# A two-layer encoder trunk on one core: one queue for the opening, and two turns of each feed-forward issued from ScalarE

## The chip, the core and the metric

The kernel runs on one NeuronCore of one Trainium2 chip. A core has five engines with a list of instructions each, which run side by side and wait for one another on semaphores: TensorE (PE, matmuls and transposes), VectorE (DVE), ScalarE (ACT), GpSimd (POOL) and SyncE (SP), which here only issues DMAs. SP and ACT have a DMA queue each (q1 and q10 in the profile); both feed the same 16 DMA engines. The metric is the time of one execution in microseconds on the device; lower is better. Times inside the program are given in us from the start of the profiled span.

## What is computed

The trunk has two layers over 256 rows (frames) of 1024 features. Each layer is a feed-forward with half weight, a mixer (convolution and attention side by side, merged by gates), and a second such feed-forward. Cut to what the change touches:

```python
D_MODEL = 1024; SEQ = 256; DEPTH = 2; D_FF = 2816
def _rms_norm(x, g):
    y = x * lax.rsqrt(jnp.mean(x * x, axis=-1, keepdims=True) + EPS)
    return y * g
def _swiglu(h, w_gate, w_up, w_down):
    return (jax.nn.silu(h @ w_gate) * (h @ w_up)) @ w_down
for l in range(DEPTH):
    x = x + 0.5 * _swiglu(_rms_norm(x, ffn1_norm[l]), ffn1_w_gate[l], ffn1_w_up[l], ffn1_w_down[l])
    ...  # mixer
    x = x + 0.5 * _swiglu(_rms_norm(x, ffn2_norm[l]), ffn2_w_gate[l], ffn2_w_up[l], ffn2_w_down[l])
```

## The kernel before

**Tiles and units.** The 256 rows are two tiles (t = 0, 1) of 128. A feed-forward runs over 11 chunks (NCH, c = 0 to 10) of 256 of the 2816 inner columns. Weights come in units of 128 partitions x 2048 floats, 1 MB each. A chunk has three units: gate and up for rows 0 to 511 of the features (half h = 0), the same for rows 512 to 1023 (h = 1), and down. A feed-forward is 33 units. Units 0 and 1 are chunk 0's gate and up, 2 and 3 chunk 1's, 4 is chunk 0's down, then 5, 6 (chunk 2's), 7 (chunk 1's down), and so on. In each half-unit of the opening, a quarter (q = 0, 1) is two blocks of 128 feature rows.

**Every product is three.** Weights and activations are float32 and each is split into a rounded part (whi, hThi, gThi) and its rest (wlo, hTlo, gTlo). TensorE forms hi x hi, hi x lo and lo x hi. So a unit goes through: a DMA into one of three raw slots (SP, `place`, L360), rounding on ACT (`split`, L1044, semaphore whi_ready), the rest on DVE (`split`, L1390, semaphore wlo_ready), and then the matmuls. SP may send unit u when wlo of unit u - 3 is done, since that frees the slot. The rounding of unit u waits for its landing and for a slot among six rounded ones (unit_free).

**The turn.** What a chunk gives (silu of gate times up, one 128 x 256 tile per t) must be transposed before the product with down. ACT splits its 32-bit words into two planes of 16 bits (`split_planes`, L1110), a DMA transpose turns both tiles at once (`plane_turn`, L385, issued by SP), DVE joins the planes again (`join`, L1478), ACT rounds (`round_joined`, L1118), DVE forms the rest gTlo (`rest_joined`, L1395), and PE may start the products with down. Chunks 0 to 9 are turned so, 40 in all over the four feed-forwards. Chunk 10 is turned by TensorE (`turn`, L716), since nothing is left to cover the DMA. Each turn waits for the join of the one before, as planes and turned are single buffers.

**Order.** Each engine's order is written out by hand, nothing is scheduled. PE does gate_up of chunk c for both tiles (24 matmuls each), then down of chunk c - 1 for both (12 each). At the end it does gate_up of chunk 10 for tile 0, half of that for tile 1, turn of chunk 10 for tile 0, down of chunk 9 for tile 0, down of chunk 10 for tile 0. ACT's `first` (L1130) has, behind the silu of tile 1 of chunk 0, the split of unit 4 and then the planes of tile 1. SP sends the turn of chunk c - 2 between the two gate-up units of chunk c and the down unit; the turn of chunk 9 is sent where the next part's first unit has been sent: after the gain, vec, qkg and first w_in loads of the mixer (L429), or after the first unit of the next layer (L400).

**The opening.** x comes in four pieces of 128 x 512. Tile 0's first piece is SP's first DMA, the second comes from ACT (L1350). Units 0 and 1 are sent in quarters, gate by SP and up by ACT (`first_unit`, L329), and x's second tile by both (`second_tile`). TensorE turns x by 128 x 128 blocks (L645), ACT rounds these with the gain as scale (`gained_round`, L1071), DVE forms the rest (`gained_rest`, L1440). PE's `first_gate_up` (L689) takes for each half tile 0 in two quarters, then tile 1 in one piece of four blocks. `keep_busy` is a number of matmuls on zeros whose result nobody reads. `factors` turns the gains into columns.

## Time and profile before

| | |
|---|---|
| runs shown, us | 1063.89, 1064.58, 1068.48; median 1064.58 |
| profiled execution, us | 1062.78, span 1060.9 |
| TensorE matmul busy | 1048.6 us (99%), 5100 instructions |
| VectorE, ScalarE, GpSimd busy | 673.2 us (63%), 560.1 us (53%), 229.5 us (22%) |
| DMA | 205.06 MB, mean 193 GB/s; q1 (SP) 61.3%, q10 (ACT) 1.2% of 16 engines' span |
| granted TensorE clock, mean over the span | 1.0 of full speed |
| split of a unit, ACT L1044 | 178 times, mean 1908 ns |
| low part of a unit, DVE L1390 | 154 times, mean 2286 ns |

How to read it: with an engine at 99% of the span, the time outside its work is what can still be saved. It has to be looked for in single places, where PE stood and something else released it. Busy time of the others tells only whether they have room; how they are ordered decides when PE gets its operands.

### The profile page before, as it was taken

What the parts mean: (1) busy time and instruction counts of PE and PEld (TensorE: products, weight loads), DVE (VectorE), ACT (ScalarE), POOL (GpSimd) and SP (SyncE); (2) the same over time, 40 slices, a digit from 0 to 9 for tenths busy, and PEclk for the clock granted to TensorE, in tenths of its full rate; (3) what the DMA queues carried; (4) which work ended last, traced back from release to release, by engine and by line L of the source; (5) the groups of instructions that cost most, each with busy time, mean ns of one, the idle gap of its engine ahead of it and who ended that gap; (6) DMA issues with size and microseconds to landing.
All of it is one profiled execution on the core that took longest, in us unless ns stands there. A gap on an engine that the chain in (4) does not pass through costs nothing. (4 is left out here: it accounts for less than half of the span.)

```text
span 1060.9 us, 13912 instructions
## 1 busy us (share of the span) xinstructions
PE 1048.6 (99%) x5100; PEld 878.8 (83%) x5100; DVE 673.2 (63%) x899; ACT 560.1 (53%) x732; POOL 229.5 (22%) x258
## 2 busy tenths in 40 slices
PE   8999999999999999999999999999999999999998
PEld 5888887998888888888888888879988887888887
DVE  6556556599976465565656546556999665564563
ACT  6445445575762554454455535536767535454461
POOL 1840000049850000000048000002589300000000
PEclk9999999999999999999999999999999999999999
DMA  8776786365645367767656686674366345867761
GB/s 277 220 230 202 211 242 225 127 219 169 208 149 179 95 203 218 225 200 219 217 159 204 186 249 204 206 247 157 132 209 232 105 159 129 220 203 220 225 203 48
DMA packets 176701, 205.06 MB, mean 193 GB/s; under 512 B 49264, under 2 KB 147856, under 8 KB 176656
## 3 DMA queue, kind: packets, MB, share of 16 engines
q1 hardware_dynamic: 174064, 200.78, 61.3%
q10 hardware_dynamic: 2592, 3.69, 1.2%
q8 instruction: 27, 0.44, 0.2%
q14 instruction: 18, 0.15, 0.0%
HBM read 192.90 MB, written 1.05 MB: 183 GB/s over the span
## 5 line engine op out<-in xcount | busy, mean ns | idle before, releaser
L1390 DVE TENSOR_TENSOR wlo<-raw,whi 128x2048 fp32r<-128x2048 f32 x154 | 351.4, 2286 | 69.1 <-ACT whi L1044 69.0
L604 PE MATMUL bank<-whi,hThi 128*128 128x512 f32 (+1 forms) x976 | 379.2, 388 | 0.3 <-DVE wlo L1390 0.3
L606 PE MATMUL bank<-whi,hTlo 128*128 128x512 f32 (+1 forms) x976 | 373.7, 383 | 0.0
L605 PE MATMUL bank<-wlo,hThi 128*128 128x512 f32 (+1 forms) x976 | 373.6, 383 | 0.0
L1044 ACT ACTIVATE whi<-raw 128x2048 fp32r<-128x2048 f32 x178 | 338.7, 1908 | 16.2 <-DMA raw<-in_ffn_w_up 7.9
L604 PEld LDWEIGHTS bank<-whi,hThi 128*128 128x128 f32 x976 | 183.4, 188 | 36.0 <-DVE wlo L1390 0.7
L606 PEld LDWEIGHTS bank<-whi,hTlo 128*128 128x128 f32 x976 | 183.2, 188 | 35.8
L605 PEld LDWEIGHTS bank<-wlo,hThi 128*128 128x128 f32 x976 | 183.5, 188 | 34.2
L1118 ACT ACTIVATE gThi<-vtok 128x512 fp32r<-128x512 f32 x40 | 25.3, 632 | 277.1 <-DVE vtok L1478 237.8
L604 PE MATMUL bank<-whi,gThi 128*128 128x512 f32 (+1 forms) x416 | 162.7, 391 | 2.7 <-DVE gTlo L1395 2.7
L605 PE MATMUL bank<-wlo,gThi 128*128 128x512 f32 (+1 forms) x416 | 161.2, 387 | 0.0
L606 PE MATMUL bank<-whi,gTlo 128*128 128x512 f32 (+1 forms) x416 | 161.2, 387 | 0.0
L472 POOL TENSOR_TENSOR small<-small,expo 128x1 f32<-128x1 f32 (+3 forms) x20 | 21.7, 1087 | 602.6 <-DVE small L1399 562.5
L1478 DVE COPY vtok<-qkT 128x1024 uint16<-128x1024 uint16 x40 | 30.2, 755 | 166.6 <-DMA qkT<-qkT 166.4
L586 POOL TENSOR_TENSOR wlo<-raw,whi 128x2048 fp32r<-128x2048 f32 x24 | 110.2, 4604 | 19.1 <-ACT whi L1044 18.8
L1557 DVE SCALAR_TENSOR_TENSOR bank<-cu,vec,bank 128x256 f32<-128x256 f32 x240 | 97.3, 484 | 0.1
L604 PEld LDWEIGHTS bank<-whi,gThi 128*128 128x128 f32 x416 | 78.1, 188 | 19.7 <-DVE gTlo L1395 4.3
L606 PEld LDWEIGHTS bank<-whi,gTlo 128*128 128x128 f32 x416 | 78.1, 188 | 16.1
L605 PEld LDWEIGHTS bank<-wlo,gThi 128*128 128x128 f32 x416 | 78.2, 188 | 15.3
L1110 ACT ACTIVATE qkT<-gates 128x512 uint16<-128x512 uint16 x80 | 50.0, 625 | 23.9 <-DVE gates L1465 23.9
L1101 ACT ACTIVATE gates<-bank,small 128x256 f32<-128x256 f32 x88 | 40.5, 460 | 19.1 <-PE bank L606 17.8
L1395 DVE TENSOR_TENSOR gTlo<-vtok,gThi 128x512 fp32r<-128x512 f32 x40 | 27.7, 692 | 35.5 <-ACT gThi L1118 35.5
(163 smaller groups left out, 805.8 us busy)
## 6 DMA issues: line engine op xcount, KB each, us to landing
raw<-in_ffn_w_down SPq DMA_DIRECT2D x88, 512.0 KB, 5.4
raw<-in_ffn_w_gate SPq DMA_DIRECT2D x86, 512.0 KB, 4.2
raw<-in_ffn_w_up SPq DMA_DIRECT2D x86, 512.0 KB, 5.3
raw<-in_w_in SPq DMA_DIRECT2D x48, 512.0 KB, 4.9
raw<-in_w_out SPq DMA_DIRECT2D x16, 512.0 KB, 4.4
raw<-in_w_in SPq DMA_DIRECT2D x8, 544.0 KB, 7.6
raw<-in_w_mla_out SPq DMA_DIRECT2D x8, 512.0 KB, 3.9
raw<-in_w_conv_out SPq DMA_DIRECT2D x8, 512.0 KB, 4.8
```

The lines of the kernel that those rows point to most:

```text
L586: nc.gpsimd.tensor_tensor(wlo[:, slot(u, RING), 0:n], raw[:, slot(u, RAW), 0:n], whi[:, slot(u, RING), 0:n].bitcast(F32), ALU.subtract).th ...
L604: nc.tensor.matmul(out, lh, rh, start=start, stop=False, skip_group_check=skip)
L605: nc.tensor.matmul(out, lh, rl, start=False, stop=False, skip_group_check=skip)
L606: return nc.tensor.matmul(out, ll, rh, start=False, stop=stop, skip_group_check=skip)
L1044: nc.scalar.activation(whi[:, slot(u0, RING), 0:USED[u0]], raw[:, slot(u0, RAW), 0:USED[u0]], ACT.Copy).then_inc(whi_ready, 1)
L1101: nc.scalar.activation(sgate[:, t, :], bank[:, 4 + t, 0:FC], ACT.Silu, scale=rs[:, t:t + 1]).then_inc(silu_ready, 1)
L1110: nc.scalar.activation(planes[:, :, :, t, :], words, ACT.Copy).then_inc(planes_ready, 1)
L1118: nc.scalar.activation(gThi[:, (c0 % 2) * 2:(c0 % 2) * 2 + 2, :], g_turned.rearrange("p (k n) -> p k n", k=2), ACT.Copy).then_inc(ghi, 2)
L1390: nc.vector.tensor_tensor(wlo[:, slot(u0, RING), 0:n], raw[:, slot(u0, RAW), 0:n], whi[:, slot(u0, RING), 0:n].bitcast(F32), ALU.subtract) ...
L1395: return nc.vector.tensor_tensor(out, in_, hi.bitcast(F32), ALU.subtract)
L1478: nc.vector.tensor_copy(g_turned.bitcast(U16).rearrange("p (n b) -> p b n", b=2), turned.rearrange("p (b j) r -> p b (j r)", b=2)).then_in ...
L1557: ins = nc.vector.scalar_tensor_tensor(out=o, in0=i, scalar=w, in1=o, op0=ALU.mult, op1=ALU.add)
```

## The change

**Opening, DMAs.** SP issues all of x and all of units 0 and 1; ACT issues none of them and keeps only the two small loads of gains. The order is: x tile 0 half 0, quarter (0, 0) as gate and up, x tile 1 half 0, quarter (0, 1), x tile 0 half 1, quarter (1, 0), x tile 1 half 1, quarter (1, 1). A new semaphore x_second marks x tile 1 half 0.

**Opening, order of work.** Each quarter is used for tile 0 and then for tile 1. For tile 1 the term with hTlo comes last. The transposes of x are now four at a time (`first_turn`), each into a bank of its own per tile (`norm_bank`). ACT and DVE alternate a half of a tile of x and a quarter of a unit. keep_busy between the first transposes and the next has 10 matmuls in place of 5. The squares of tile 0 on DVE (`first_squares`) go from its first place to behind the first quarter of unit 1.

**Turns.** The turns of chunks 0 and 9 of each feed-forward (8 of 40) are issued by ACT, right behind the planes. In `first` the planes of tile 1 and the turn stand ahead of the split of unit 4, not behind it. The turns of chunks 1 to 8 stay with SP.

```diff
@@ x and units 0 and 1, on SP
-        def first_unit(eng, h, g):
-        def second_tile(eng, h):
...
+            def x_half(t, h, landed):
+                sp.dma_start(x[:, t, h * 512:(h + 1) * 512],
+                             a["x"][0, t * P:(t + 1) * P, h * 512:(h + 1) * 512]).then_inc(landed, 16)
+            def first_quarter(h, q, landed):
+                u0 = unit_gu(0, 0, h)
+                dst = raw[:, slot(u0, RAW), 0:2048].rearrange("p (k g n) -> p k g n", k=4, g=2)
+                rows = slice((4 * h + 2 * q) * P, (4 * h + 2 * q + 2) * P)
+                sp.wait_ge(wlo_ready, u0 + 1)
+                for g, w in enumerate((wg[0], wu[0])):
+                    sp.dma_start(dst[:, 2 * q:2 * q + 2, g, :],
+                                 w[0, rows, 0:FC].rearrange("(k p) n -> p k n", p=P)).then_inc(landed, 16)
...
-                        first_unit(sp, 0, 0)
-                        second_tile(sp, 0)
-                        first_unit(sp, 1, 0)
+                        for h in range(2):
+                            if h:
+                                x_half(0, 1, x_landed[0])
+                            first_quarter(h, 0, first_landed[h])
+                            x_half(1, h, x_landed[1] if h else x_second)
+                            first_quarter(h, 1, raw_landed[slot(unit_gu(0, 0, h), RAW)])
@@ turns no longer on SP
-                        if f == 0:
-                            plane_turn(l - 1, 1, NCH - 2)
...
-                    if c > 1:
+                    if c > 2:
                         plane_turn(l, f, c - 2)
...
-                    if h == 1:
-                        plane_turn(l, 0, NCH - 2)
...
-            plane_turn(DEPTH - 1, 1, NCH - 2)
@@ first_products(t, h, q) on PE
+                    term(hThi, whi, first=True)
+                    if t == 0:
+                        pe.wait_ge(nlo, per_norm_half(0, 0, t, h))
+                        term(hTlo, whi)
...
+                    ins = term(hThi, wlo, last=t == 0)
+                    if t == 1:
+                        pe.wait_ge(nlo, per_norm_half(0, 0, t, h))
+                        ins = term(hTlo, whi, last=True)
@@ first_gate_up on PE
+                            ins = first_products(0, h, q)
+                            if (h, q) == (0, 1):
+                                first_turn(1, 1)
+                                turn_factors(1)
+                            elif (h, q) == (1, 1):
+                                ins.then_inc(gu_done, 1)
+                            ins = first_products(1, h, q)
+                            if (h, q) == (0, 0):
+                                first_turn(0, 1)
...
-                        norm(l, n, 0)
-                        keep_busy(5)
+                        first_turn(0, 0)
+                        keep_busy(10)
+                        first_turn(1, 0)
@@ turns on ACT
+                def plane_turn(c):
+                    act.wait_ge(planes_ready, per_turn(l, f, c) * TT)
+                    act.wait_ge(joined, per_turn(l, f, c))
+                    act.dma_start_transpose(turned[:, :, :], planes.rearrange("p b k t f -> p (b k t f)")
+                                            ).then_inc(turned_landed, 16)
...
                     silu(0, 1)
+                    split_planes(0, 1)
+                    plane_turn(0)
                     split(l, UB[f] + 4)
-                    split_planes(0, 1)
...
                 pair(NCH - 2, NCH - 2)
+                plane_turn(NCH - 2)
@@ ACT's opening
-            act.dma_start(x[:, 0, 512:D], a["x"][0, 0:P, 512:D]).then_inc(x_landed[0], 16)
...
-            first_unit(act, 0, 1)
-            second_tile(act, 1)
-            first_unit(act, 1, 1)
...
+                    for h in range(2):
+                        gained_round(0, 0, 0, h)
+                        first_split(h, 0)
+                        gained_round(0, 0, 1, h)
+                        first_split(h, 1)
@@ DVE's opening
+                    for h in range(2):
+                        gained_rest(0, 0, 0, h)
+                        first_split(h, 0)
+                        if h:
+                            first_squares()
+                        gained_rest(0, 0, 1, h)
+                        if h:
+                            norm_scale(0, 0, 0)
+                        first_split(h, 1)
```

How it moves instructions. TensorE's list from the first transposes of x to the first transposes of its second tile, before (bank<-ident,x is a transpose of x, bank<-zero is keep_busy, L676 are the first products):

```order
L645 MATMUL bank<-ident,x 128x128 x8
L611 MATMUL bank<-zero 128x512 x5
L676 MATMUL bank<-whi,hThi 128x512 x2
L676 MATMUL bank<-whi,hTlo 128x512 x2
L676 MATMUL bank<-wlo,hThi 128x512 x2
```

And the same place in the changed kernel, where these lines have the numbers L683, L618 and L692:

```order
L683 MATMUL bank<-ident,x 128x128 x4
L618 MATMUL bank<-zero 128x512 x10
L683 MATMUL bank<-ident,x 128x128 x4
L692 MATMUL bank<-whi,hThi 128x512 x2
L692 MATMUL bank<-whi,hTlo 128x512 x2
L692 MATMUL bank<-wlo,hThi 128x512 x2
L692 MATMUL bank<-whi,hThi 128x512 x2
L692 MATMUL bank<-wlo,hThi 128x512 x2
L692 MATMUL bank<-whi,hTlo 128x512 x2
```

Four transposes of tile 0 have left the place ahead of the products, four of tile 1 have come there, and tile 1 follows tile 0 on the same quarter. ScalarE's list around chunk 0 of a feed-forward before (gates<-bank is silu, qkT<-gates are the planes, whi<-raw of 2048 a split of a unit):

```order
L1101 ACTIVATE gates<-bank,small 128x256
L1052 ACTIVATE htok,small<-x 128x1024
L1044 ACTIVATE whi<-raw 128x2048
L1110 ACTIVATE qkT<-gates 128x4x128
L1101 ACTIVATE gates<-bank,small 128x256
L1044 ACTIVATE whi<-raw 128x2048
L1110 ACTIVATE qkT<-gates 128x4x128
```

And now, with the waits printed, in the changed kernel:

```order
L1124 ACTIVATE gates<-bank,small 128x256 [waits rs_ready,gu_done]
L1074 ACTIVATE htok,small<-x 128x1024 [waits x_landed1,x_second,x_new]
L1065 ACTIVATE whi<-raw 128x2048 [waits unit_free,raw_landed0]
L1133 ACTIVATE qkT<-gates 128x4x128 [waits gu_ready]
L1124 ACTIVATE gates<-bank,small 128x256 [waits rs_ready,unit_free]
L1133 ACTIVATE qkT<-gates 128x4x128 [waits gu_ready]
L1140 DMA_TRANSPOSE qkT<-qkT 128x8x128 [waits joined,planes_ready]
L1065 ACTIVATE whi<-raw 128x2048 [waits unit_free,raw_landed1]
```

The second planes have moved ahead of the second split, and the issue of the turn stands between them. SyncE's list at the start of a mixer loses the turn of chunk 9 between the two pairs of w_in; before:

```order
L360 DMA raw<-in_w_in 128x2x544 x2
L385 DMA_TRANSPOSE qkT<-qkT 128x8x128
L360 DMA raw<-in_w_in 128x2x544 x2
```

## Rows read from the trace of the kernel before

**Rows 1.** Waits of TensorE, whole span: us in total, times, longest us.
```profile
PE bank L604 <- DVE gTlo L1395: 2.7, 4, 0.8
```

**Rows 2.** Timeline of the opening: start us, us, engine, work [idle before <-releaser].
```profile
3.76 1.73 PE L645 MATMUL bank<-ident,x 128*128 128x128 f32 x8
...
5.18 0.84 ACTq L1341 DMA_DIRECT2D cacc<-in_ffn_norm  x1
...
5.33 1.24 PE L611 MATMUL bank<-zero 128*128 128x512 bf16 x5
...
6.35 1.14 ACT L1071 ACTIVATE hThi<-bank,fgain 128x128 fp32r<-128x128 f32 x4
...
7.91 1.06 ACT L1063 ACTIVATE whi<-raw 128x1024 fp32r<-128x1024 f32 x1 [0.42 <-DMA raw<-in_ffn_w_up]
8.99 1.22 DVE L1424 TENSOR_TENSOR wlo<-raw,whi 128x1024 fp32r<-128x1024 f32 x1 [0.34 <-ACT whi L1063]
...
9.11 0.70 PE L676 MATMUL bank<-whi,hThi 128*128 128x512 f32 x2 [2.53 <-ACT whi L1063]
```

**Rows 3.** Timeline, end of the opening's products and turn of chunk 0.
```profile
20.50 0.48 ACT L1101 ACTIVATE gates<-bank,small 128x256 f32<-128x256 f32 x1 [1.27 <-PE bank L676]
...
22.12 1.07 PE L676 MATMUL bank<-wlo,hThi 128*128 128x512 f32 x4
...
26.06 0.48 DVE L1465 SCALAR_TENSOR_TENSOR gates<-bank,small,gates 128x256 f32<-128x256 f32 x1
...
26.20 0.50 PE L604 MATMUL bank<-whi,hThi 128*128 128x512 f32 x1 [0.29 <-DVE wlo L1390]
...
26.54 2.29 DVE L1390 TENSOR_TENSOR wlo<-raw,whi 128x2048 fp32r<-128x2048 f32 x1
...
32.73 0.76 DVE L1478 COPY vtok<-qkT 128x1024 uint16<-128x1024 uint16 x1 [3.90 <-DMA qkT<-qkT]
...
35.15 0.50 PE L604 MATMUL bank<-whi,gThi 128*128 128x512 f32 x1 [0.49 <-DVE gTlo L1395]
```

**Rows 4.** Timelines by engine, turn of chunk 9, layer 1's first feed-forward.
```profile
689.99 0.61 ACT L1110 ACTIVATE qkT<-gates 128x512 uint16<-128x512 uint16 x1
...
690.84 3.40 SPq L385 DMA_TRANSPOSE qkT<-qkT  x1
...
700.07 0.75 DVE L1478 COPY vtok<-qkT 128x1024 uint16<-128x1024 uint16 x1 [4.30 <-DMA qkT<-qkT]
...
702.78 0.44 PE L716 MATMUL bank<-ident,gates 128*128 128x128 f32 x2 [1.59 <-DVE gates L1465]
...
706.65 0.50 PE L604 MATMUL bank<-whi,gThi 128*128 128x512 f32 x1 [0.68 <-DVE gTlo L1395]
```

**Rows 5.** Timelines by engine, the same turn in layer 0.
```profile
168.86 2.23 SPq L385 DMA_TRANSPOSE qkT<-qkT  x1
...
176.91 0.75 DVE L1478 COPY vtok<-qkT 128x1024 uint16<-128x1024 uint16 x1 [3.94 <-DMA qkT<-qkT]
...
183.50 0.50 PE L604 MATMUL bank<-whi,gThi 128*128 128x512 f32 x1 [0.68 <-DVE gTlo L1395]
```

**Rows 6.** Timelines by engine, turns of chunk 0: layer 1's first, then last feed-forward.
```profile
556.87 0.39 PE L604 MATMUL bank<-whi,gThi 128*128 128x512 f32 x1
...
888.26 0.48 DVE L1465 SCALAR_TENSOR_TENSOR gates<-bank,small,gates 128x256 f32<-128x256 f32 x1
...
890.27 1.25 SPq L385 DMA_TRANSPOSE qkT<-qkT  x1
...
899.09 0.50 PE L604 MATMUL bank<-whi,gThi 128*128 128x512 f32 x1 [0.80 <-DVE gTlo L1395]
```

**Rows 7.** Source line of the turns: issue in ns, then landing, min/median/max.
```profile
L385 SPq DMA_TRANSPOSE qkT<-qkT x40: 1232/2048/3403, 27.2 to 1032.9; - x40
...
DMA to landing us min/median/max: 3.0/6.2/9.2
```

**Rows 8.** Stretch 5 to 12 us: busy of engines, PEclk, DMA share, GB/s.
```profile
5.00:12.00 7.00, 4.47 (x19) 2.35 (x17) 4.47 (x9) 4.47 (x11) 0.00 (x0) 1.00 1.05 353
```

More of the change, by code:

```diff
@@ L194, in trunk @@
         x_first = sem("x_first")
+        x_second = sem("x_second")
         gain_landed = sem("gain_landed")
@@ L670, in gate_up, with first_turn @@
                             between()
-                def first_products(t, u, ks, wait_rest, wait_low):
-                    def term(left, right, k, start, stop):
-                        return nc.tensor.matmul(bank[:, 4 + t, :], left[:, 4 * u + k, t * P:(t + 1) * P],
-                                                view(right, u, 2048, 4)[:, k, :], start=start, stop=stop)
-                    for k in ks:
-                        term(hThi, whi, k, u == 0 and k == 0, False)
-                    wait_rest()
-                    for k in ks:
-                        term(hTlo, whi, k, False, False)
-                    wait_low()
-                    for k in ks:
-                        ins = term(hThi, wlo, k, False, u == 1 and k == 3)
+                def first_turn(t, h):
+                    pe.wait_ge((x_first, x_second)[t] if h == 0 else x_landed[t], 16)
+                    if h:
+                        pe.wait_ge(nlo, per_norm_half(0, 0, t, 0))
+                    for k in range(4):
+                        ins = nc.tensor.transpose(bank[:, norm_bank(0, 0, t, h), k * P:(k + 1) * P],
+                                                  x[:, t, (4 * h + k) * P:(4 * h + k + 1) * P], ident[:, :])
+                    ins.then_inc(ntr, 1)
@@ new lines, in first_products, with term @@
+                def first_products(t, h, q):
+                    def term(left, right, first=False, last=False):
+                        for k in (2 * q, 2 * q + 1):
+                            ins = nc.tensor.matmul(bank[:, 4 + t, :], left[:, 4 * h + k, t * P:(t + 1) * P],
+                                                   view(right, h, 2048, 4)[:, k, :],
+                                                   start=first and (h, k) == (0, 0), stop=last and (h, k) == (1, 3))
+                        return ins
+                    pe.wait_ge(nhi, per_norm_half(0, 0, t, h))
+                    if q == 0:
+                        pe.wait_ge(first_hi, h + 1)
+                    else:
+                        pe.wait_ge(whi_ready, h + 1)
+                    term(hThi, whi, first=True)
+                    if t == 0:
+                        pe.wait_ge(nlo, per_norm_half(0, 0, t, h))
+                        term(hTlo, whi)
+                    if q == 0:
+                        pe.wait_ge(first_lo, h + 1)
+                    else:
+                        unit_waits(pe, 0, h)
+                    ins = term(hThi, wlo, last=t == 0)
+                    if t == 1:
+                        pe.wait_ge(nlo, per_norm_half(0, 0, t, h))
+                        ins = term(hTlo, whi, last=True)
```

60 lines of the change are left out of this document (12 added, 48 removed).

## The prediction, made before the changed kernel ran

> **What bounds the kernel now.** I read the shares of the page first: TensorE (PE) is busy 1048.6 us of a span of 1060.9, so this change can win only what PE does not work. Next the waits of PE alone over the whole span [rows 1]: nearly all of it in four waits for gTlo, 2.7 us. Beside them the timeline shows 2.53 us before the first product [rows 2] and 1.59 us for the product to be turned in layer 1 [rows 4]. To the idle time of such a row 0.16 us are added, because matmuls stand 0.227 us apart while their modelled length is 0.39 (four in 1.07, [rows 3]); the four gTlo waits and the last named then cost 0.65, 0.84, 0.84, 0.96 and about 1.6 us. Everything else is TensorE's own pace. So two places count: the opening up to 35.15 us, and the turn (DMA transpose) of the first and the last-but-one chunk of a feed-forward.
>
> **Opening, the start.** PE's first useful matmul begins at 9.11 us [rows 2]. Behind it stands ACT: its queue issued eight transfers before it computed, the last from 5.18 to 6.02 us, so the first rounding of x (1.14 us for four tiles) starts at 6.35 although its transposes lay in PSUM by 4.9; then the first split of weights waited for the up quarter until 7.91. In the changed kernel ACT issues two small transfers, and SP sends everything. Rounding then starts at 4.9 and ends at 6.0. Ahead of the first pair of quarters' end there are 768 KB (half a tile of x, gate, up). The chip moved 353 GB/s from 5 to 12 us [rows 8]: three quarters of a MB at that rate take 2.2 us; from about 2.5 us and with half a us for landing I estimate 5.2, and up to 6 with a slow start. The split (1.06) is then done at 7.0 to 7.1. But PE is not there yet: keep_busy grows from 5 to 10 matmuls. They begin at 4.6, where PE's transposes still stand 0.21 apart (8 in 1.73), two at 0.42, the rest at the 0.22 of [rows 2] (5 in 1.24), so until 7.1; four transposes follow. First product at 7.6: 1.5 us earlier than now, and it is PE's own list that sets it, which also covers a landing up to 0.5 us late.
>
> **Opening, the middle.** One pass over a quarter for one tile is six matmuls, 1.37 us; eight passes are 10.9 us, with 12 transposes and the factor's in between 1.5 us. Per quarter, with its two passes of 1.37, ACT has one group of roundings and one split, 1.14 + 1.06 = 2.2 us, DVE as long a group and 1.22, 2.35 us, and once the squares, about one split more [rows 2]. Both keep up, with stalls of some 0.2 us where the rest of x for tile 1 comes last (that is why its term is put last). I get the end of the first products at 20.2 (7.6 + 10.9 + 1.5 + 0.2). Before, it is 23.03 (four matmuls from 22.12, [rows 3]). The second unit's low part is ready at 20.45 (DVE's chain from 14.6: squares, group, 1.22, 2.29, each about as now), so chunk 1 begins at 20.5, **2.5 us early**.
>
> **Opening, what is late next.** This does not stay. Silu of tile 0 sits on ACT ahead of the split of unit 3, and from its start at 20.50 to the first product with unit 3 at 26.20 there are 5.7 us [rows 3]. In the changed kernel tile 0's gate_up ends at 18.9 instead of 20.3, so silu starts at 19.1 and unit 3 is ready at 24.8; PE arrives at 23.2 and stands 1.6 us. **1.4 us early** is left. Then comes the turn: the product of tile 1 follows that low part by 0.4 us as at 26.06 now (25.2), its planes take 0.6 (25.8), the issue on ACT, t = 1.25 us (27.1), the split of unit 4, 1.90 (29.0), its low part, 2.29 (31.3), and only then DVE's join, since the split stands ahead of it in DVE's list; join to first product is 32.73 to 35.15, 2.42 us. That gives 33.7, against 33.0 at which PE is there and 35.15 now: **opening 1.45 us**. The turn itself has landed by then (25.8 + 5.5 as now = 31.3).
>
> **Price of an issue on ACT.** No row shows a turn issued there. On SP it takes 1.23 to 3.40 us, 2.05 in the middle [rows 7]. The long ones stand behind loads of weights in the same queue; at 1.25 [rows 6] SP had issued nothing for a while. ACT's queue is empty outside the mixer, so I take 1.25 and keep 3.4 as upper end. It pushes the split that follows and its low part on DVE, and through them the join.
>
> **Last-but-one turns (four).** In layer 1's first feed-forward SP issues vectors, gains and w_in, then the turn at 690.84, which takes it 3.40 us; it lands 9.2 us later, DVE starts at 700.07, PE waits 1.6 us for the product and 0.84 for gTlo [rows 4]. The planes are ready at 690.6. From ACT: issue to 691.9, split 1.9, low part 2.3, so the join can start at 696.1 if the turn lands within 5.5 us. That is 3.9 us earlier. The product of the last chunk then waits only for its own matmuls: PE is at the turn at 701.0 (702.78 less 1.75) and done with tile 0 twelve matmuls before, at 698.3; silu and mul, half a us each, are over at 699.5: both stalls go, **2.4 us**. In layer 0 the same turn is issued at 168.86 and joined from 176.91 on [rows 5]; the join comes at 174.3 instead, and the 0.84 us before 183.50 go: **0.85 us**. In the two second feed-forwards no wait of PE hangs on it ([rows 1] has four gTlo waits in all, and all four are named here): gain and loss zero; if an issue of 3.4 us pushed them, some us lie between gTlo and its use.
>
> **First turns (the other three).** The planes are split before unit 4's split instead of after it, 0.86 us earlier: in the last feed-forward mul is done at 888.74 [rows 6], planes at 889.4, issue to 890.65, split, low part to 894.9; join no later than 895.8 is needed for PE at 898.13, and the turn lands by then even with the present 6.4 us. The 0.96 us before 899.09 go: **0.95 us**. The other two have no wait now; by the same sum their gTlo comes at 374.1 and 555.9, where PE wants it at 375.0 and 556.9. Slack 0.9 us each, so t up to 2.2 is free (PE's row of the second is in [rows 6]). Unit 7's load is issued 2.8 us later than now in each; ACT wants it some 11 us after that.
>
> **Sum.** 1.45 + 2.4 + 0.85 + 0.95 = 5.65 us, against the profiled execution: 1062.78 (span 1060.9) to 1057.1. That execution was 1.8 us below the median of the runs shown, 1064.58; the same difference from the median gives 1059.0 us. As a function of t: gain = 6.9 - t up to 2.2 us, and 13.5 - 4t above, because four first turns then lie on PE's path; from 2.8 on the last-but-one turns give less too. It is zero near 3.2.
>
> **A rule against it.** The layer-1 turn stood 9.2 us behind other loads [rows 4]; the sum takes it that a queue of its own ends this. DMA: Bandwidth & Descriptors of the Trainium skill (Issuing engines are not separate DMA queues) says that transfers started by different engines run on the same 16 DMA engines and interleave, so only the sequencer's time is saved; the same page (Queues, rings and completion order) says that each engine goes round the queues packet by packet. By the second the turn passes the waiting loads, as the sum has it; by the first it would land little sooner, and the sum would be that of rival (1). No row here decides it.
>
> **Rivals.**
> (1) The turns land no sooner from ACT, because their packets share the engines with w_in. For: the chip is busy there. Against: the turn that had little else beside it landed in 3.0 us, the best of forty [rows 7]. Then 2.4 + 0.85 fall away: gain 2.4, 1062.2 us. Chance 0.15.
> (2) The opening wins nothing: a single queue brings the first quarters as late as now (7.9), the first product is at 9.1, and everything in the opening shifts by 1.5 us. Gain 4.2, 1060.4 us. For: today two queues fill the start, and one may not. Against: later, SP's queue alone carries all weights, and the two share the engines now. Chance 0.12.
> (3) **Slower**: the issue on ACT is long, as SP's longest, 3.4 us or more. Then the first turns of all four feed-forwards are late through split, low part and join, more than the last-but-one turns give back: at 3.4 the opening loses 0.7, two first turns 1.2 each and the last 0.25, the last-but-one still give 2.25: 1.1 us slower, 1065.7 us, and 4 to 6 us more per us beyond. It decides from t = 3.2. Against: ACT's queue holds nothing else. Chance 0.06.
> (4) The opening keeps its 2.5 us, because split and low part of unit 3 run into less: gain 6.7, 1057.9 us. Chance 0.10.
>
> **How the numbers follow.** The forecast has 0.57, with its own range 4.4 to 6.8 us of gain, 1057.8 to 1060.2. Faster by over 0.5% (5.3 us; about what a measurement of this kernel can tell from no change) means below 1059.3: rather more than two thirds of the forecast's part and all of (4), 0.50. Within 0.5%: the rest of it, (1), (2) and most of (3), 0.45. Slower 0.05. The range leaves out the ends of (3) and (4) and allows for the spread of the runs, 1063.9 to 1068.5 before: 1056.0 to 1064.5.
>
> **What would show it.** First product at 7.6 (late landing: over 8.5); chunk 1's first matmul at 20.5 and a wait of 1.6 us before unit 3; down of chunk 0 at 33.7. A turn's issue on ACT of 1.2 to 1.3 us. No wait of PE for the product in layer 1, none for gTlo at the last-but-one turns and the last feed-forward. Wrong would be: PE waits for gTlo or the low part of unit 4 in the middle feed-forwards, or a turn from ACT landing after 7 us.

## The result, and the profile of the changed kernel

The changed kernel takes 1071.22 us (median of 20 runs, 1058.41 to 1075.74) against 1063.96 (20 runs of the kernel before, 1060.25 to 1068.48). The ratio is 1.0059, 95% interval 1.0043 to 1.0075: slower by 0.6%, where 1059.0 was forecast. The profiled execution took 1072.15 us with a span of 1070.3; that of the kernel before had a span of 1060.9. Two of the 20 runs (1058.41 and 1062.65 us, mean granted clock 1.000 and 0.998 against 0.995 in the profiled one) show little or nothing of the loss; they left no trace that would say why.

TensorE's waits over the whole span (us in total, times, longest):

```profile
PE bank L736 <- DVE gates L1492: 9.2, 2, 4.8
PE bank L611 <- DVE gTlo L1421: 1.2, 2, 0.7
...
PE bank L611 <- DVE wlo L1416: 1.0, 1, 1.0
PE bank L683 <- DMA x<-in_x: 1.0, 1, 1.0
```

Two of the four gTlo waits of [rows 1] are gone; the forecast had a third one gone too, that of the last feed-forward. In their place stand two waits for the product that PE is to turn, 9.2 us together, or 4.6 and 5.0 with the 0.16 us that the prediction adds to each. Both stand ahead of a mixer, where the turn of chunk 9 is under way. Timelines by engine there, layer 0 and then layer 1 (start us, us, engine, work, idle before and its releaser):

```profile
168.60 2.12 ACTq L1140 DMA_TRANSPOSE qkT<-qkT  x1
...
170.40 5.88 SPq L355 DMA_DIRECT2D raw<-in_w_in  x4
...
181.06 0.74 DVE L1505 COPY vtok<-qkT 128x1024 uint16<-128x1024 uint16 x1 [6.00 <-DMA qkT<-qkT]
...
183.76 0.69 PE L736 MATMUL bank<-ident,gates 128*128 128x128 f32 x2 [4.43 <-DVE gates L1492]
...
696.36 2.87 ACTq L1140 DMA_TRANSPOSE qkT<-qkT  x1
...
709.20 0.74 DVE L1505 COPY vtok<-qkT 128x1024 uint16<-128x1024 uint16 x1 [5.62 <-DMA qkT<-qkT]
...
711.89 0.69 PE L736 MATMUL bank<-ident,gates 128*128 128x128 f32 x2 [4.79 <-DVE gates L1492]
```

From issue to join are now 12.5 and 12.8 us; in [rows 5] and [rows 4] they were 8.1 and 9.2. The turn is issued right behind its planes as before, and from issue to join it takes 4.4 and 3.6 us longer. DVE's mul of the last chunk stands behind this join in DVE's list, and PE's transpose of that product stands ahead of the last products with down: so all of PE waits.

The wait costs more than itself. Stretches around the two places (busy us of PE with its instructions in brackets, then the other engines; behind them the granted clock, DMA share, GB/s):

```profile
179.00:184.00 5.00, 0.57 (x3) 0.24 (x2) 1.83 (x3) 2.12 (x3) 0.00 (x0) 0.85 0.90 206
184.00:190.00 6.00, 6.00 (x17) 4.79 (x17) 5.09 (x3) 2.96 (x3) 0.00 (x0) 0.56 0.25 66
190.00:200.00 10.00, 10.00 (x51) 8.30 (x51) 3.48 (x5) 2.25 (x5) 0.57 (x1) 1.00 0.40 146
706.00:712.00 6.00, 1.21 (x6) 0.67 (x5) 1.82 (x3) 1.98 (x3) 0.00 (x0) 0.96 1.00 255
712.00:716.00 4.00, 4.00 (x13) 3.25 (x14) 3.05 (x3) 3.10 (x3) 0.00 (x0) 0.63 0.05 19
716.00:726.00 10.00, 10.00 (x47) 8.20 (x46) 5.52 (x6) 2.01 (x4) 0.57 (x1) 1.00 0.55 184
...
183.70:185.70 2.00, 1.94 (x6) 1.66 (x7) 0.89 (x2) 2.00 (x3) 0.00 (x0) 0.50 0.04 11
711.90:713.90 2.00, 2.00 (x6) 1.71 (x7) 0.95 (x1) 2.00 (x3) 0.00 (x0) 0.50 0.12 43
```

Right behind each wait the granted clock is 0.50, the lower of its two levels (1.2 of 2.4 GHz); the stretches of 6 and 4 us hold 0.56 and 0.63 because it rises to 1.00 within them. In 184 to 190 there are 17 matmuls where the next stretch has 30.6 per 6 us, so 13.6 matmuls' time, 2.7 us, is missing; in 712 to 716 there are 13 against 18.8, which is 1.2 us. Waits of 9.5 and clock of 3.9 make 13.4 us. Less the waits that were there before (1.6 + 0.84 + 0.84 at the same two places) some 10 us are left. The spans of the two executions differ by 9.4, so these two places account for the whole loss.

The opening, in rows of its timeline:

```profile
4.84 1.14 ACT L1093 ACTIVATE hThi<-bank,fgain 128x128 fp32r<-128x128 f32 x4 [1.21 <-PE bank L683]
5.86 1.07 ACT L1085 ACTIVATE whi<-raw 128x1024 fp32r<-128x1024 f32 x1
...
8.07 0.66 PE L683 MATMUL bank<-ident,x 128*128 128x128 f32 x4 [0.95 <-DMA x<-in_x]
8.49 0.71 PE L692 MATMUL bank<-whi,hThi 128*128 128x512 f32 x2
...
21.84 0.47 PE L611 MATMUL bank<-whi,hThi 128*128 128x512 f32 x1 [0.37 <-DVE gates L1492]
...
25.84 0.50 PE L611 MATMUL bank<-whi,hThi 128*128 128x512 f32 x1 [1.02 <-DVE wlo L1416]
...
34.86 0.50 PE L611 MATMUL bank<-whi,gThi 128*128 128x512 f32 x1 [0.54 <-DVE gTlo L1421]
```

Rounding at 4.84 and the split over by 6.93 came as forecast (4.9 and 7.0). But x's tile 1, half 0, landed at 8.03 (of its 16 completion marks in the trace the first came at 5.72), and its four transposes stand ahead of the first product: 8.49 instead of 7.6. All later steps are 1.0 to 1.3 us behind the forecast: chunk 1 at 21.84 (20.5), unit 3 at 25.84 (24.8), down of chunk 0 at 34.86 (33.7; before 35.15). The wait before unit 3 is 1.02 us, where 1.6 was forecast.

The page of the line of ACT's turns (issue in ns, then landing in us, minimum, median, maximum):

```profile
L1140 ACTq DMA_TRANSPOSE qkT<-qkT x8: 1256/1298/2870, 26.9 to 1042.3; - x8
...
DMA to landing us min/median/max: 3.1/6.1/12.8
```

The issue costs ACT 1.3 us, as taken (t = 1.25). It is the landing that goes above 12 us: 12.4 us in layer 0, 12.8 in layer 1.

### The profile page after: what moved, and what is told of

Read it like the earlier page. It is cut to its first block, busy times and chain, and to the rows that moved or that the text cites. A ratio compares the mean times of both kernels' runs of the same rounds, so it can differ in the third digit from the quotient of the medians.

```text
span 1070.3 us, 13927 instructions
## 1 busy us (share of the span) xinstructions
PE 1052.8 (98%) x5105; PEld 882.1 (82%) x5105; DVE 672.5 (63%) x899; ACT 561.9 (52%) x732; POOL 230.7 (22%) x258
## 4 chain that ended last, share of the span: by engine, by line
PE 91%; DMA 4%; ACT 2%; DVE 1%; issue 1%; ACTq 0%; POOL 0%; SPq 0%; DVEq 0%
PE bank L611 28%; PE bank L612 28%; PE bank L613 28%; DMA qkT<-qkT 3%; PE bank L692 1%; ACT whi L1065 1%; PE bank L650 1%; PE bank L844 1%; PE bank L856 1%; DMA x<-in_x 1%; ACT htok L1074 0%; PE bank L876 0%; PE bank L877 0%; PE bank L855 0%; PE bank L1030 0%
```

## Experiments

The span of one profiled execution is a poor measure here, because the opening scatters from execution to execution: the down of chunk 0 begins anywhere between 35.15 and 37.65 us in five profiled executions with the old opening (e4, with chunk 0's turn on ACT, among them), and between 34.28 and 36.83 in eight with the new (three of them with chunk 0's turn on SP). The table therefore has, beside the ratio, the part from there to the end of the span (span less the start of that row), and the time from the end of the turn's planes to the start of its join in layers 0 and 1. Span and what stands right of it are from one execution each.

| kernel | median us | ratio to before, 95% | span | down of chunk 0 at | rest | planes to join, us |
|---|---|---|---|---|---|---|
| before | 1063.96 | 1 | 1060.9 | 35.15 | 1025.8 | 8.1, 9.5 |
| changed | 1071.22 | 1.0059 [1.0043, 1.0075] | 1070.3 | 34.86 | 1035.4 | 12.5, 12.9 |
| e1_last_on_sp | 1062.74 | 0.9993 [0.9979, 1.0008] | 1058.5 | 35.16 | 1023.3 | 6.6, 9.1 |
| e2_opening_only | 1062.68 | 0.9991 [0.9976, 1.0007] | 1057.1 | 34.74 | 1022.4 | 6.4, 8.0 |
| e3_last_only | 1073.46 | 1.0086 [1.0070, 1.0102] | 1074.0 | 37.56 | 1036.4 | 13.3, 12.8 |
| e4_first_only | 1063.63 | 1.0006 [0.9990, 1.0021] | 1063.8 | 37.65 | 1026.2 | 9.2, 9.0 |
| e5_hold_w_in | 1059.57 | 0.9990 [0.9977, 1.0003] | 1055.5 | 34.28 | 1021.2 | 6.5, 7.0 |
| e6_vec_later | 1059.09 | 0.9985 [0.9968, 1.0003] | 1055.3 | 34.31 | 1021.0 | 5.6, 5.6 |
| e7_hold_vec_later | 1058.55 | 0.9969 [0.9957, 0.9980] | 1057.7 | 36.72 | 1021.0 | 5.7, 5.6 |
| e8_sp_vec_later | 1058.51 | 0.9968 [0.9956, 0.9980] | 1056.9 | 34.69 | 1022.2 | 4.9, 7.5 |
| e9_turn_behind | 1069.35 | 1.0060 [1.0041, 1.0080] | 1069.1 | 35.27 | 1033.8 | 11.5, 12.4 |
| e10_vec_only | 1059.60 | 0.9976 [0.9961, 0.9990] | 1057.8 | 36.50 | 1021.3 | 5.5, 5.0 |
| e11_x_ahead | 1059.00 | 0.9968 [0.9955, 0.9980] | 1057.9 | 36.83 | 1021.1 | 4.5, 4.5 |

Three groups were run, each with its own runs of the kernel before beside it: e1 to e4 (1063.47), e5 to e8 (1061.36), e9 to e11 (1061.72, on another chip than the other runs). Medians of different groups are not compared, ratios are.

### Which part loses: e1 to e4

**e1_last_on_sp.** The changed kernel with the turns of chunk 9 back on SP at their old places:

```diff
                 pair(NCH - 2, NCH - 2)
-                plane_turn(NCH - 2)
...
                 for h in range(2):
+                    if h == 1:
+                        plane_turn(l, 0, NCH - 2)
                     block_of(l, UM + M_PR + h, a["w_in"], 4 * h * P, 4, O1, PR)
```

> The changed kernel with the turns of chunk 9 issued by SyncE again, in their old places; opening and the turns of chunk 0 stay as changed. Theory (shared engines): the changed kernel lost its time at two turns alone, those of chunk 9 ahead of a mixer, which landed 12.5 and 12.8 us after their issue on ScalarE (8.0 and 9.2 from SyncE before), because SyncE's w_in load that used to stand behind them in one queue now runs beside them. Then this kernel has no wait of TensorE over 2 us at the product to be turned and ends near the kernel before, from 3 us under it to 1 us over: ratio 0.997 to 1.001. Rival (opening or turns of chunk 0 cost the time): it stays 4 us or more over the kernel before, ratio 1.004 or more.

Measured 0.9993 [0.9979, 1.0008], as the theory has it, and the longest PE wait for the product is 1.1 us. The other three are the kernel before with one part each. **e2_opening_only** has the opening's DMAs and PE, ACT and DVE order of the change, all turns on SP:

> The kernel before with the changed opening alone; all 40 turns from SyncE at their old places. In the changed kernel the down product of chunk 0 began at 34.86 us against 35.15, so the opening looks worth 0.3 us with the turn of chunk 0 on ScalarE. Theory: on its own it is worth 0 to 1.5 us, ratio 0.9985 to 1.0; with the turn back on SyncE the first split of unit 4 is earlier. Rival (the rearranged opening also shifts later loads so that turns land later): over 1.002.

Measured 0.9991 [0.9976, 1.0007]: inside the theory's range, and not told from no change. **e3_last_only** has the turns of chunk 9 on ACT (the lines of e1's diff the other way round):

> The kernel before with the four turns of chunk 9 issued from ScalarE and nothing else. Theory: this part alone carries the whole loss: turns ahead of the mixers land 12 to 13 us after issue, TensorE waits 4 to 5 us at the product to be turned in both layers and then runs some 12 matmuls 0.43 us apart; 8 to 10 us slower than before, ratio 1.008 to 1.0095. Rival (the loss needs the opening or the turns of chunk 0 beside it, through a shifted phase of loads): under 1.003. The prediction's own view was 3 us faster, 0.997.

Measured 1.0086 [1.0070, 1.0102], with waits of PE of 5.4 and 4.9 us for the product to be turned, as expected. **e4_first_only** has the turns of chunk 0 on ACT, with the planes ahead of unit 4's split:

> The kernel before with the four turns of chunk 0 issued from ScalarE, planes ahead of the split of unit 4, nothing else. Issue 1.25 to 1.35 us. Theory: it lands no sooner than from SyncE (5.6 to 7.1 us), the split of unit 4 comes 2.9 us later, the slack of 0.5 to 1 us is used up, TensorE gains nothing: 0 to 1 us slower, ratio 1.000 to 1.001. Rival (as predicted): the wait before the down product of the last feed-forward goes, 1 us faster, 0.999.

Measured 1.0006 [0.9990, 1.0021]; the turns land 5.7 to 6.8 us after their issue. So the loss is the move of chunk 9's turns, it is there without the opening and the first turns, and nothing is seen of a worth of the turns of chunk 0. One thing does not add up: the move alone costs 1.0086, the whole change 1.0059, each beyond the other's interval. The opening (0.9991) makes good a third of that; the rest is not explained.

### Why the turn lands late: e5 to e8

Two things stand out in the trace of the changed kernel. First, the turn was issued at 168.60, and for nearly five us not one packet of ACT's queue (q10) moves; nor does much else. DMA of the stretch 168.6 to 173.5 (busy tenths of the engines in 40 slices, GB/s in the same slices, then packets, MB and share of the one queue that has any):

```profile
DMA  9622110000000000000022539798999999999999
GB/s 291 184 75 85 38 28 10 4 6 8 5 8 4 6 12 8 14 10 16 16 46 67 138 133 315 273 392 322 463 355 409 391 409 426 409 444 373 462 373 409
...
q1 hardware_dynamic: 800, 0.91, 51.7%
```

From about 169 to 171 the DMA engines are nearly idle. What trickles there are the q and k norm rows, which SP issued from 165.02 on, each sent to all 128 partitions: the trace has 128-byte packets, 24 to 53 in each half us. This is no different in the kernel before: its turn was issued at 168.86 and had its first packet at 174.55, and from 169.5 to 171.5 its engines moved 17 GB/s. Second, when q10's packets come, they run beside the second unit of w_in, which SP issued from 170.40 on; in the kernel before the turn stood ahead of that unit in the same queue. This is new. Stretch 174 to 177.5 of the changed kernel, then 179 to 183 of e3_last_only (queue: packets, MB, share):

```profile
q1 hardware_dynamic: 532, 1.09, 89.0%
q10 hardware_dynamic: 531, 0.14, 20.2%
```

```profile
q1 hardware_dynamic: 697, 1.31, 86.9%
q10 hardware_dynamic: 716, 0.18, 21.1%
```

Both queues get nearly the same number of packets, 532 to 531 and 697 to 716; but q1's have up to 2176 bytes and q10's 256, so the turn gets about an eighth of the bytes. In layer 1 the counts are less even (339 to 509 in 702 to 706 of the changed kernel). Theory A is this sharing, theory B the small loads.

**e5_hold_w_in** takes the sharing away: SP sends the second unit only when the turn has landed.

```diff
                 for h in range(2):
+                    if h == 1:
+                        sp.wait_ge(turned_landed, per_turn(l, 0, NCH - 2) * 16)
                     block_of(l, UM + M_PR + h, a["w_in"], 4 * h * P, 4, O1, PR)
```

> The changed kernel; ahead of the second w_in unit of each mixer SyncE now waits until the turn of chunk 9 has landed. In the changed kernel that unit was issued 1.8 us after the turn and ran beside it; the DMA engines gave each queue one packet in turn (697 packets of SyncE's queue to 716 of ScalarE's in 4 us of the run with the last turns alone on ScalarE), 2176-byte packets against 256-byte ones. Theory A (equal packets, and the unit behind is what the turn shares with): the turn lands 7.5 to 9.5 us after issue as it did from SyncE, the waits of 4.8 and 4.4 us shrink under 2 us, ratio 0.998 to 1.002. Theory B (small loads ahead, vec and the q and k norms, hold the start of the turn's packets, 5 us after issue): the landing hardly moves, over 11 us, ratio 1.005 or more.

```profile
167.99 1.86 ACTq L1142 DMA_TRANSPOSE qkT<-qkT  x1
174.47 0.76 DVE L1507 COPY vtok<-qkT 128x1024 uint16<-128x1024 uint16 x1 [0.28 <-DMA qkT<-qkT]
178.58 0.38 PE L738 MATMUL bank<-ident,gates 128*128 128x128 f32 x2
```

The join comes 6.5 us after the issue (7.0 in layer 1), PE does not wait (no idle time on its row), and the ratio is 0.9990. This is theory A's ratio, with a landing still sooner than its 7.5 us, and against theory B.

**e6_vec_later** takes the small loads away instead: the vector row and the q and k norms go behind both units, and the sharing is left possible.

```diff
-                sp.wait_ge(vec_used, l + 1)
-                sp.dma_start(vec[:, :], a["vec"][l]).then_inc(vec_landed, 16)
-                for n, w in enumerate((a["q_norm"], a["k_norm"])):
-                    sp.dma_start(qkg[:, n, :], w[bass.ds(l, 1), NOPE:QK].to_broadcast([P, ROPE])).then_inc(vec_landed, 16)
                 for h in range(2):
                     block_of(l, UM + M_PR + h, a["w_in"], 4 * h * P, 4, O1, PR)
+                sp.wait_ge(vec_used, l + 1)
+                sp.dma_start(vec[:, :], a["vec"][l]).then_inc(vec_landed, 16)
+                for n, w in enumerate((a["q_norm"], a["k_norm"])):
+                    sp.dma_start(qkg[:, n, :], w[bass.ds(l, 1), NOPE:QK].to_broadcast([P, ROPE])).then_inc(vec_landed, 16)
```

> The changed kernel with the loads of vec and of the q and k norms sent behind the two w_in units of the mixer instead of ahead of them. In the trace of the changed kernel the DMA engines moved next to nothing for 2 us while these loads' 128-byte packets went out, and the turn's first packet came 5 us after its issue. Theory B: packets of the turn start 1.5 to 3 us after issue, landing 6 to 9 us, ratio 0.997 to 1.002. Theory A (only the unit beside it counts): the small loads cost 1 to 2 us at most, the turn still shares with 2.2 MB of w_in and lands after 10 us or more, ratio 1.003 to 1.006.

```profile
168.03 1.27 ACTq L1141 DMA_TRANSPOSE qkT<-qkT  x1
173.56 0.75 DVE L1506 COPY vtok<-qkT 128x1024 uint16<-128x1024 uint16 x1
```

Its queues in 168.6 to 171.6:

```profile
q10 hardware_dynamic: 1056, 0.26, 56.3%
q1 hardware_dynamic: 201, 0.40, 52.9%
```

Now q10's first packet comes 1.2 us after the issue, q10 has over half of the engines' time in this stretch, the issue is the short one, and the join starts without idle time in front of it: DVE's own list, not the landing, sets it. In the trace the turn has landed at 171.66, 3.6 us after its issue, sooner than the 6 us of theory B. Alone, this experiment would have been taken for theory B; e5 shows that holding the unit back is enough too.

**e7_hold_vec_later** has both edits, **e8_sp_vec_later** has e6's edit with all turns on SP (opening as changed).

> Both edits on the changed kernel: small loads behind the w_in units, and the second unit held until the turn has landed. Whatever the parts are, both theories together leave the turn little beside it: landing 4 to 6 us after issue, no wait of TensorE for the product to be turned, 2 to 4 us faster than the kernel before, ratio 0.996 to 0.998. If it stays above 1.001 there is a third cause in ScalarE's queue itself.

> The changed opening, all turns from SyncE at their old places, and the small loads behind the two w_in units of the mixer. The turn of chunk 9 then stands behind one w_in unit alone. Theory B: it lands 4.5 to 6 us after issue instead of 8 to 9, both waits before the last chunk's products go (0.8 us in layer 0, 2.4 us in layer 1), ratio 0.995 to 0.998 against the kernel before, 2 to 3 us under the run with the opening alone. Theory A: the turn is behind w_in as before, landing 7 us or more, ratio as with the opening alone, 0.999.

Both measured the same, 0.9969 and 0.9968: 0.3% faster than the kernel before. With e11 they have the lowest ratios of the study. In e8's layer 1 the issue still took 3.11 us and the join came 7.5 us after it, longer than theory B had it, but no PE wait hung on it. The two causes act in series rather than add up: without the sharing planes-to-join falls from 12.5 to 6.5 us, without the small loads to 5.6, without both to 5.7.

Where the turn's packets stand among those of w_in can be counted in the traces. A turn has 1024 packets of 256 bytes, each w_in unit 512 of 2176. Layer 0, then layer 1:

| kernel | first packet of the turn after its issue, us | w_in packets started before it | from its first to its last packet, us |
|---|---|---|---|
| before | 5.7, 5.5 | 449, 313 | 1.8, 3.2 |
| changed | 5.2, 4.2 | 431, 286 | 6.4, 7.9 |
| e3_last_only | 5.3, 4.8 | 145, 294 | 7.4, 7.2 |
| e5_hold_w_in | 3.5, 2.8 | 428, 384 | 2.4, 3.6 |
| e6_vec_later | 1.2, 1.2 | 462, 470 | 1.9, 2.1 |
| e7_hold_vec_later | 3.0, 2.3 | 457, 451 | 1.9, 1.8 |
| e9_turn_behind (below) | 5.1, 5.1 | 922, 856 | 2.6, 3.6 |

The change left the first packet nearly where it was and stretched the rest from 1.8 and 3.2 us to 6.4 and 7.9: this is the loss. It also shows that ACT's queue did not take the turn past the first unit, which SP had issued before. In layer 0 of e7, with no small loads in the way, the turn was issued at 170.44, 0.12 us before the first packet of that unit moved, and its own first packet still came at 173.40, behind 457 of the 512. So the small loads need not hold ACT's queue themselves; they hold up the first unit, and the turn's packets come when a good part of that unit has gone (more than half, in all rows but those of e3). In e6 it was nearly gone 1.2 us after the issue, and the turn was through before the second unit's packets came. Which engine issues the turn makes no difference that e7 and e8 show, once the small loads are out of the way.

### Which order in one queue: e9 to e11

**e9_turn_behind** asks whether a second queue is needed for the harm at all: the kernel before, the turn moved on SP from ahead of the second unit to behind it.

```diff
                 for h in range(2):
-                    if h == 1:
-                        plane_turn(l, 0, NCH - 2)
                     block_of(l, UM + M_PR + h, a["w_in"], 4 * h * P, 4, O1, PR)
+                    if h == 1:
+                        plane_turn(l, 0, NCH - 2)
```

> The kernel before, with one line moved: SP still issues the turn of chunk 9 in the mixers, but behind the second unit of w_in instead of ahead of it. Asks whether the place against that unit alone costs, with no second queue in it. Theory (order on the line, not the queue's owner, decides): the turn's packets come behind all of that unit, so issue to join is 8 to 11 us from the issue, and the issue itself comes later by the two issues of the unit; the join is at 180 us or later in layer 0 and 708 or later in layer 1 (before: 176.91 and 700.07), TensorE stands 3 to 6 us at each of the two products, loss 4 to 10 us, 1066 to 1072 us where before gives 1062.5, ratio 1.004 to 1.009. Rival (a second queue is what hurts, the packets of two queues in turn): within one queue the turn loses at most 2 us, TensorE stands under 1.5 us each, ratio 1.000 to 1.002. The first feed-forward's other turns are as before.

```profile
172.18 1.92 SPq L385 DMA_TRANSPOSE qkT<-qkT  x1
180.48 0.74 DVE L1478 COPY vtok<-qkT 128x1024 uint16<-128x1024 uint16 x1 [7.35 <-DMA qkT<-qkT]
183.18 0.69 PE L716 MATMUL bank<-ident,gates 128*128 128x128 f32 x2 [3.41 <-DVE gates L1465]
...
710.69 0.44 PE L716 MATMUL bank<-ident,gates 128*128 128x128 f32 x2 [4.29 <-DVE gates L1465]
```

1.0060 [1.0041, 1.0080], as the theory has it: a loss like that of the change (1.0059), with one queue only. The closer comparison is e3, which also has nothing but the move, to ACT: 1.0086 [1.0070, 1.0102], the intervals just overlap, so a second queue may cost a little more. Planes to join are 11.5 and 12.4 us here, 12.5 and 12.9 in the changed kernel. A turn that ACT's own queue got at 168.60 is no sooner joined (181.06) than one that SP issued at 172.18 behind both units (180.48). The ways differ, since here the turn is issued 3.3 us later than before and then comes in one piece behind the unit, and in the changed kernel it is spread among the unit's packets. What costs is to leave the place ahead of that unit.

**e10_vec_only** is the kernel before with e6's edit alone.

> The kernel before with its old opening and all turns on SP, and only the four small loads at the start of a mixer (vector row, q and k norms) sent behind both units of w_in. Theory (these small packets hold what stands behind them): the turns of chunk 9 land 4.8 to 7.5 us after their issue, as in the variant that has the same edit under the new opening; TensorE no longer stands 1.6 us for the product in layer 1 nor 0.8 us before the last product's low part; worth 2.4 to 3.3 us, ratio 0.9968 to 0.998. Rival (the gain of 0.3% of that variant is the opening's): ratio 0.9985 to 1.0005 here.

```profile
170.21 1.23 SPq L385 DMA_TRANSPOSE qkT<-qkT  x1
175.71 0.75 DVE L1479 COPY vtok<-qkT 128x1024 uint16<-128x1024 uint16 x1 [1.39 <-DMA qkT<-qkT]
...
690.56 1.23 SPq L385 DMA_TRANSPOSE qkT<-qkT  x1
695.54 0.75 DVE L1479 COPY vtok<-qkT 128x1024 uint16<-128x1024 uint16 x1 [0.87 <-DMA qkT<-qkT]
```

0.9976 [0.9961, 0.9990]. In [rows 4] the issue alone took 3.40 us and the join came 9.2 later; here 1.23 and 5.0. The theory's range is met. (In layer 1 of e8 the same edit left the issue at 3.11 us, so the length of the issue is not the small loads' alone.) So most of the gain that the forecast put on "a queue of its own" (2.4 + 0.85 us) was to be had, 0.24% or 2.5 us, by moving three small loads of each mixer (the vector row and two norms; the expectation says four). What e8 has more, 0.0008 or 0.8 us, is within the intervals, so no worth of the opening can be read from it.

**e11_x_ahead** tests the opening's first term, on top of e8: x's tile 1, half 0, is sent right behind tile 0's.

```diff
             x_half(0, 0, x_first)
+            x_half(1, 0, x_second)
...
-                            x_half(1, h, x_landed[1] if h else x_second)
+                            if h:
+                                x_half(1, 1, x_landed[1])
```

> The changed opening with all turns on SP and the small loads behind w_in, and one DMA moved: the first half of x's tile 1 goes right behind the first half of tile 0, ahead of quarter (0, 0). In the changed opening this piece came at about 8.0 us, behind 768 KB, and TensorE's transposes of it stood ahead of the first product. Theory (the opening's first term was lost to that landing): the piece lands by 5 us, the quarter 0.7 us later than now at about 6.4, the first product begins at 7.6 to 8.0 instead of 8.2 to 8.5. Whether that comes through is the second question: if the opening is held by the order of its dependencies, chunk 1 begins 0.5 to 0.8 us earlier than 21.84; if it is held by the rate at which the 9 MB of the first units arrive, it begins within 0.2 us of that and the ratio is that of the same kernel without the move, 0.9968 within its interval of 0.0012.

```profile
7.32 0.60 PE L692 MATMUL bank<-ident,x 128*128 128x128 f32 x4
...
7.85 1.06 ACT L1094 ACTIVATE whi<-raw 128x1024 fp32r<-128x1024 f32 x1 [1.91 <-DMA raw<-in_ffn_w_up]
...
9.05 0.70 PE L701 MATMUL bank<-whi,hThi 128*128 128x512 f32 x2 [1.13 <-ACT whi L1094]
```

The piece landed at 5.03, as expected, but the quarter that is behind it at 7.83, 1.4 us later than expected, and the first product began at 9.05. The wait has changed its name from x to the weights. Chunk 1 begins at 23.43 and the down of chunk 0 at 36.83, later than either side of the expectation had it, in an execution at the late end of the scatter. The ratio, 0.9968, is e8's, so the move is worth nothing that can be told. It is not the mean rate that holds the first product: the engines moved 1.7 MB between 2.5 and 8 us here. Of the 32 completion marks of the quarter's two DMAs the first came at 4.76, the last but one at 7.08 and the last at 7.83. Why single shares come so late is open.

## Why the prediction was wrong

**Last-but-one turns: the step that failed.** It said: from ACT the join can start at 696.1 "if the turn lands within 5.5 us". This condition was given no lower side. The sum, and rival (1) as well, let the landing be at worst as late as now; that it could become later was in no case, since only the issue was thought of as moved. But on SP's list the turn stood ahead of the second unit of w_in [rows 4], and taking it from there gave that unit the place beside it. SP issued it 1.8 us after the turn, before the turn's first packet. The other half of the step failed too: the turn did not pass the first unit either, its first packet came 5.2 and 4.2 us after the issue (5.7 and 5.5 before). Measured: issue to join 4.4 and 3.6 us longer instead of shorter, which is some 10 us lost (waits, and 3.9 us of lower clock behind them, a term that the sum did not have) where +3.25 was forecast. That is 13 us. Between the profiled executions the error is 15 us (1072.15 against 1057.1), and the opening and the first turns have the other 2; against the medians it is 12.2.

**The choice under "A rule against it".** I let the second of two sections of DMA: Bandwidth & Descriptors (the Trainium skill) decide, "each engine goes round the queues packet by packet", and concluded that the turn passes what waits. The traces agree with the rule in layer 0 (532 packets to 531 in the changed kernel, 697 to 716 in e3; that the engines change over after every single packet is not shown) and not with the conclusion. The rule shares packets, and a queue of small ones gets few bytes: 0.18 of 1.49 MB. And the turn's packets did not begin among the waiting ones of the first unit, but behind 431 (layer 0) and 286 (layer 1) of their 512. The same section (Queues, rings and completion order) states that SP and ACT have rings of their own but no descriptor generator of their own; that would fit a turn that stays behind a unit issued on the other queue, and no run here shows that it is the reason. The first section (Issuing engines are not separate DMA queues), that only the sequencer's time is saved, was the better guide, and still too kind: the landing was not unchanged, it was later by 4.4 and 3.6 us.

**Rival (3)** had the sign right by luck, with another mechanism: an issue on ACT of over 3.2 us. Two issues did take 2.12 and 2.87 us, but neither was on PE's path, which waited for the landing. The median, 1.3 us, was right.

**First turns: forecast 0.95 us, none seen.** The stall at the last feed-forward stays, 0.69 us in the row where 0.80 stood [rows 6]:

```profile
908.57 0.50 PE L611 MATMUL bank<-whi,gThi 128*128 128x512 f32 x1 [0.69 <-DVE gTlo L1421]
```

The planes are 0.86 us earlier, but from issue to join it is 7.1 us, where 6.4 was taken from before; the gain goes into the landing. In e4 the same stall is 0.38. The ratio of e4, 1.0006 within 0.0015, agrees with zero and barely admits 0.95 us.

**Opening: ACT's part right, the start of PE wrong, the size not shown by the one trace.** ACT's rounding and split came as worked out. The term that was missed is the landing of x's tile 1. The sum counted 768 KB ahead of the split, but PE's own list has four transposes of the next 256 KB ahead of the first product, and their landing was put at nothing. It also used the 353 GB/s of [rows 8] from 2.5 us on. In the changed kernel the DMAs brought less in these microseconds:

```profile
5.00:6.00 1.00, 1.00 (x6) 0.49 (x5) 0.00 (x0) 1.00 (x5) 0.00 (x0) 1.00 0.87 216
6.00:7.00 1.00, 1.00 (x6) 0.29 (x3) 0.98 (x4) 0.93 (x1) 0.00 (x0) 1.00 0.80 187
7.00:8.00 1.00, 0.12 (x1) 0.00 (x0) 1.00 (x2) 0.00 (x0) 0.00 (x0) 1.00 0.77 274
```

Against the profiled execution of before, the opening wins 0.3 us at the down of chunk 0. But that one was the earliest of five with the old opening: 35.15, 35.27, 36.50, 37.56, 37.65, mean 36.4. The seven executions with the changed one (without e11) have 34.28, 34.31, 34.69, 34.74, 34.86, 35.16, 36.72, mean 35.0. That is 1.5 us, what was forecast, though from few executions that scatter by 2.5; the timed e2 says 1.0 us with an interval of 1.6 to either side, so neither zero nor 1.45 is excluded.

**"No wait of PE for the product in layer 1"** and **"a turn from ACT landing after 7 us"** were named as what would decide, and they did: the wait was 5.0 us, and the turns landed after 12.4 and 12.8.

What stays open: why a turn from ACT's queue stays behind a good part of a unit that SP issued before it, and why the norm rows trickle with the engines nearly idle. The slow stretch moves with the rows: in e6, where they come behind the w_in units, it is at 695.5 to 696.5 (34 GB/s).

## What to carry to other kernels

A DMA in a queue has a place, and moving it to another queue gives up that place: before costing the move, look at what stood behind it in the old queue, since this will now run beside it. Do not count on a new queue to take it past what was issued earlier, either. In this kernel the urgent transfer of small packets was helped by what was issued around it (the large transfer behind it held back, or the small loads ahead of it moved behind) and not by a queue of its own. And where TensorE comes to stand for several us, add what the clock takes after it; here 4 us on top of waits of 9.5.

## What the runs showed of the hardware

- Two queues on the same 16 engines got like numbers of packets, 532 to 531 in 3.5 us and 697 to 716 in 4 us, at 1.31 against 0.18 MB in the second. A transpose with 256-byte packets beside a load with 2176-byte ones took 12 to 13 us to its join; without that load beside it, 6.5 and 7.0 (e5).
- A transpose issued on ACT's queue 0.12 us before the first packet of a load that SP had issued started behind 457 of that load's 512 packets (e7, layer 0).
- While two loads of a 128-byte row to 128 partitions were under way, all queues together moved 4 to 16 GB/s for over 2 us, where 350 to 400 are moved otherwise.
- After waits of 4.6 and 5.0 us the granted clock was 0.50 at first and 0.56 and 0.63 over the following 6 and 4 us, about 2.7 and 1.2 us of TensorE's work; after that it was 1.00 again.
- The first 35 us, with the loads of the opening in them, scatter by 2.5 us between executions with the same opening, more than the edit of it was forecast to be worth.
